# An encoder layer with grouped experts: the first expert's down rows split ahead of the second tile's columns, and three row tiles of the last norm finished on TensorE

## Chip, cores, metric

One Trainium2 chip, one core. The metric is the device time of the program in microseconds, the median of the runs.

## The reference

One layer of a hybrid encoder, 1024 tokens of width 1024, all in float32: a projection, a convolution branch and chunked attention, merged and projected, then a layer norm, then a mixture of experts and the last layer norm. The change touches the end alone:

```python
x = layer_norm(ALPHA * x + mixed, ln1_g[l], ln1_b[l])
x = layer_norm(ALPHA * x + grouped_moe(x, w_router, b_router, w_gate_up[l], w_down[l]),
               ln2_g[l], ln2_b[l])

def layer_norm(x, g, b):
    mu = jnp.mean(xf, axis=-1, keepdims=True)
    var = jnp.mean(jnp.square(xf - mu), axis=-1, keepdims=True)
    return ((xf - mu) * lax.rsqrt(var + LN_EPS)).astype(x.dtype) * g + b

# in grouped_moe: 16 experts, each token goes to 2 of them
    g, u = jnp.split(t @ w_gate_up[e], 2, axis=-1)
    out = out + combine[:, e:e + 1] * ((jax.nn.silu(g) * u) @ w_down[e])
```

## The kernel before, in words

All engines are programmed by hand, each with its own order of instructions, and meet at semaphores only. Matrices are multiplied in three products of float32 halves (a "high" part that ScalarE makes by a copy, and a "low" part that VectorE makes by subtracting the high one): high by high, high by low, low by high. Weights and activations are both split so.

**The experts.** The tokens of an expert are gathered in tiles of 128. A table `tab`, made by VectorE at run time (lines 1845 to 1855), says which expert each tile belongs to; here there are 21 tiles. `tables` (line 1862) says that it and the counts are there; `slots_ok` (line 1867) says that `w_slot` (each token's weight) and `to_i` (where its result is added) are, which are the last readers of memory that the down rows' buffers share. Every engine loads four counts into registers (`ends`, line 1235 and 1238 to 1241).

For tile i TensorE transposes the gathered rows (`transpose_x`, line 1505), multiplies the result for tile i-2 by the down weights (`down`, products of lines 1436 to 1438), transposes tile i-1's hidden values (`transpose_h`, line 1532) and multiplies by the gate and up weights (`up`, 8 chunks of rows by 3 x 2 products). The first tiles are written out one by one (lines 1561 to 1584). ScalarE copies the columns out (`x_t`, line 1634), scales the result (`y`, line 1670), copies the down rows' high part (`down_rows`, line 1645, 4 rows for each expert) and that of the transposed hidden values (`h_t`, 1651), then the next expert's gate rows (`gate_rows`, line 1330, 8 copies), then does silu (1661). VectorE follows it with the low parts (`x_t` 1790, `dn_l` 1875, `hbl` 1879, `gu` 1336) and the gate's product (`gate`, 1891).

In ScalarE's order before the change the first expert's `down_rows` stand in step(1), behind silu(0) (lines 1683 to 1690). In VectorE's order tile 1's `x_t` and three gate rows stand ahead of the slots (lines 1863 to 1867); the first `dn_l` stand in step(1), behind gate(0) and the last four gate rows (1903 to 1907).

SP loads weights in the order of lines 1304 to 1310: the gate and up rows of expert e+1 (1 MB pairs, each once the pair of two experts ago is used up), then, when `dn_lo` says that all four low parts of expert e-1 are made, the down rows of expert e (2 MB into `dn_raw`). GpSimd gathers tokens (line 1364) and adds results to memory (line 1374); it waits for `slots_ok` before its step(1) (1389 to 1391).

**The last norm.** SP reads the summed rows back in 8 row tiles (line 1318). For each, VectorE takes the mean from a column (`mean`, 1925), ScalarE squares with a sum (1710) and takes the root (1713), VectorE subtracts and multiplies by g (`scale_row`, 1932), takes the reciprocal (1938) and multiplies by it and adds b (`finish`, 1941). A ninth pass normalises the rows of the last expert tile, which VectorE adds from PSUM (`last_rows`, 1948) ahead of row tile 4; ScalarE takes their sum at its turn 6 (1708). SP stores the row tiles in order (1320 to 1321); when all are out and the ninth is ready GpSimd stores that one (1406 to 1409).

Of the kernel before, what the change touches and what calls it, by code (L numbers as in the profile page):

```python
# [13 lines left out]
P = 128  # L14
# [69 lines left out]
def encoder_layer(nc, xT, x, wblk, b_in, dw, dwb, lncg, lncb, relb, b_o, ln1_g, ln1_b,  # L84
# [5 lines left out]
    with ctx:  # L90
# [101 lines left out]
        ys2 = at("ys2", [P, D + 1], F32, 180.5)  # L192

# [990 lines left out]
def moe(nc, sem, m):  # L1184
# [7 lines left out]
     xf, g2_b, b2_b, rows_l, norm_l, ys2, squares, x1_tot, w_last, to_last, cst, eps2, st6, mv, rstd, nmr, wgt, ids_i, id_now, to_i, to_now, w_slot, tab, cum_i, ends_i, rows_i, br_b,  # L1192
     ps, psf, ident) = (m[k] for k in (
         "x1 x1t hot_a hot_b wr_t ones rt_a rt_b rank_a rank_b slot_i mh sums xgh2 xgl2 hot_0 both upto_t val wide tc id0 one_i init_p wo_add gu dn_h dn_l dn_raw xg xgh xgl hb hbh hbl ys "
         "xf g2_b b2_b rows_l norm_l ys2 squares x1_tot w_last to_last cst eps2 st6 mv rstd nmr wgt ids_i id_now to_i to_now w_slot tab cum_i ends_i rows_i br_b "
# [11 lines left out]
    idc = sem("idc"); toc = sem("toc"); to_set = sem("to_set"); slots_ok = sem("slots_ok"); id_set = sem("id_set"); gath = sem("gath")  # L1207
# [6 lines left out]
    tot_set = sem("tot_set"); f_tot = sem("f_tot"); f_nm = sem("f_nm"); f_sq = sem("f_sq"); f_sd = sem("f_sd")  # L1214
# [10 lines left out]
    logits_of = lambda a, z: ps[:, 6, (NE + 1) * a:(NE + 1) * z].rearrange("p (t e) -> p t e", e=NE + 1)  # L1225
    by_g = lambda a: a.rearrange("p (g e) -> p g e", e=EPG)
# [45 lines left out]
    def split_dn(i):  # L1272
        return {0: False, 1: True}.get(i) if isinstance(i, int) else None


    def place_of(e):

        return 1 - e % 2
# [13 lines left out]
    def sync_part(sp):  # L1292
        sp.wait_ge(x1_out, 16 * TT)
        sp.wait_ge(acc_out, 16 * TT)
        sp.wait_ge(xt_r, TT)
        load_gu(sp, 1, pairs=range(2, 4))
        sp.wait_ge(lg_done, TT)
        load_dn(sp, 0)

        sp.wait_ge(tot_set, 1)  # L1300
        sp.dma_start(acc_dram[0:SEQ, D:D + 1].rearrange("(t p) c -> p t c", p=P), x1_tot[:], allow_slow_non_contiguous=True).then_inc(acc_out, 16)
        sp.wait_ge(ids_done, 3)
        sp.wait_ge(tables, 1)
# [35 lines left out]
    def pool_part(pool):  # L1339
# [27 lines left out]
        def store(i, rows=ys[:]):  # L1367
# [5 lines left out]
            pool.sem_inc(to_set, 1)  # L1373
# [32 lines left out]
        pool.wait_ge(f_ok, TT + 1)  # L1406
# [198 lines left out]

    def halves(i):

        return [slice(HALF * h, HALF * h + HALF) for h in range(2)]
# [12 lines left out]
    def scalar_part(act):  # L1621
# [14 lines left out]
        def down_rows(i, first=False, before=None, rows=range(FC)):  # L1636
            e = 0 if first else load(act, T_E, i - 1)
            act.wait_ge(dn_in, e * 16 + 16)
            if first:

                act.wait_ge(slots_ok, 1)
            if not first:
                act.wait_ge(dn_done, i - 1 if before is None else before)
            for k in rows:
                act.activation(dn_h[:, k, :], dn_raw[:, k, :], ACT.Copy).then_inc(dn_hi, 1)  # L1645
# [26 lines left out]
        def step(i):  # L1672
# [5 lines left out]
            when(act, T_SPLIT_DN, i, split_dn(i), lambda: down_rows(i, first))  # L1678
# [6 lines left out]
        x_t(1)  # L1685
        act.wait_ge(tables, 1)
        total, end3, end2, end1 = ends(act)
        silu(0)
# [15 lines left out]
        for t in range(TT + 1):  # L1704
            if t == TT - 2:

                act.wait_ge(rows_ok, 1)
                act.activation(norm_l[:], rows_l[:, 0:D], ACT.Copy, accum_out=mv[:, TT, 0:1]).then_inc(f_tot, 1)
# [4 lines left out]
            act.activation(rstd[:, t:t + 1], mv[:, t, 1:2], ACT.Sqrt, scale=1.0 / D, bias=eps2[:]).then_inc(f_sd, 1)  # L1713

# [77 lines left out]
    def vector_part(dve):  # L1792
# [78 lines left out]
        def down_rows(i, first=False, rows=range(FC)):  # L1871
            e = 0 if first else load(dve, T_E, i - 1)
# [20 lines left out]
        def step(i):  # L1893
# [4 lines left out]
            when(dve, T_SPLIT_DN, i, split_dn(i), lambda: down_rows(i, static and i == 1))  # L1898
# [36 lines left out]
        def finish(t):  # L1935
# [3 lines left out]
            dve.wait_ge(f_rs, t + 1)  # L1939
            dve.wait_ge(f_g, t + 1)  # L1940
# [68 lines left out]
```

## Time and profile before

| | us |
|---|---|
| median of 3 runs (1184.24 to 1185.25) | 1184.93 |
| the profiled execution's own time | 1181.39 |
| its span | 1179.5 |
| TensorE busy | 1107.2 (94%) |
| VectorE, ScalarE busy | 817.9, 551.8 |
| `tables` made | 764.93 |
| first product of tile 1 | 774.91 |
| last product of the last tile begins | 1151.34 |
| last store is issued by GpSimd | 1173.54 |

PE is TensorE's products, PEld its weight loads, DVE is VectorE, ACT is ScalarE, POOL is GpSimd, SP is SyncE; a q behind a name is the engine's sequencer. A line of a timeline gives the start and the length in us, the engine, the source line, what is written and from what, how many instructions were merged, and in brackets the engine's idle time before it with what released it.

### The profile page before, as it was taken

What the parts mean: (1) busy time and instruction counts of PE and PEld (TensorE: products, weight loads), DVE (VectorE), ACT (ScalarE), POOL (GpSimd) and SP (SyncE); (2) the same over time, 40 slices, a digit from 0 to 9 for tenths busy, and PEclk for the clock granted to TensorE, in tenths of its full rate; (3) what the DMA queues carried; (4) which work ended last, traced back from release to release, by engine and by line L of the source; (5) the groups of instructions that cost most, each with busy time, mean ns of one, the idle gap of its engine ahead of it and who ended that gap; (6) DMA issues with size and microseconds to landing.
All of it is one profiled execution on the core that took longest, in us unless ns stands there. A gap on an engine that the chain in (4) does not pass through costs nothing.

```text
span 1179.5 us, 17089 instructions
## 1 busy us (share of the span) xinstructions
PE 1107.2 (94%) x5645; PEld 924.2 (78%) x5646; DVE 817.9 (69%) x1147; ACT 551.8 (47%) x814; POOL 93.0 (8%) x101
## 2 busy tenths in 40 slices
PE   7999999999999989899999999999999999999980
PEld 5888888879777778778788888778788888888760
DVE  5799999835365755566587478778678665458767
ACT  5111212233476755656333033358577555457753
POOL 0000000000000000000000000034112211112220
PEclk9999999999999999999999999799999999999985
DMA  6121332322201010071344135569999876799965
GB/s 255 54 90 45 107 92 87 108 96 66 72 19 41 19 41 1 36 289 69 129 165 161 72 143 200 182 259 383 330 308 392 312 234 217 251 331 337 351 208 218
DMA packets 49797, 199.58 MB, mean 169 GB/s; under 512 B 7248, under 2 KB 7632, under 8 KB 47680
## 3 DMA queue, kind: packets, MB, share of 16 engines
q1 hardware_dynamic: 43536, 176.19, 39.7%
q0 software_dynamic: 6192, 22.49, 7.8%
q8 instruction: 41, 0.67, 0.2%
q14 instruction: 28, 0.23, 0.1%
HBM read 166.21 MB, written 32.52 MB: 168 GB/s over the span
## 4 chain that ended last, share of the span: by engine, by line
PE 80%; DVE 6%; DMA 5%; ACT 4%; issue 4%; ACTq 0%; DVEq 0%; SPq 0%; POOL 0%; POOLq 0%
PE ps L469 17%; PE ps L471 16%; PE ps L470 16%; PE ps L1436 8%; PE ps L1438 8%; PE ps L1437 8%; DMA gu<-in_wexp 3%; PE ps L1505 1%; PE ps L1432 1%; PE ps L554 1%; PE ps L540 1%; ACT pr L801 1%; ACT pth L825 1%; DVE ptl L1043 1%; DVE xf L1932 1%
## 5 line engine op out<-in xcount | busy, mean ns | idle before, releaser
L469 PE MATMUL ps<-xh,wh 128*128 128x512 f32 x512 | 203.0, 396 | 12.2 <-DVE xl L905 8.1
L470 PE MATMUL ps<-xl,wh 128*128 128x512 f32 x512 | 200.0, 391 | 0.0
L471 PE MATMUL ps<-xh,wl 128*128 128x512 f32 x512 | 199.9, 390 | 0.0
L1336 DVE TENSOR_TENSOR gu<-gu (+1 forms) x128 | 148.6, 1220 | 34.8 <-issue 23.9
L928 DVE SCALAR_TENSOR_TENSOR cv<-u,dw_t,cv 128x1024 f32<-128x1024 f32 x120 | 154.1, 1284 | 3.7
L1436 PE MATMUL ps<-gu,xgh 128*128 x336 | 133.3, 397 | 2.0 <-DVE xgl L1790 2.0
L1330 ACT ACTIVATE gu<-gu (+1 forms) x128 | 124.4, 1048 | 21.1 <-DMA gu<-in_wexp 13.4
L1438 PE MATMUL ps<-gu,xgl 128*128 x336 | 131.1, 390 | 0.0
L1437 PE MATMUL ps<-gu,xgh 128*128 x336 | 130.8, 389 | 0.0
L469 PEld LDWEIGHTS ps<-xh,wh 128*128 128x128 f32 x512 | 96.5, 189 | 34.4 <-issue 14.4
L471 PEld LDWEIGHTS ps<-xh,wl 128*128 128x128 f32 x512 | 96.5, 188 | 20.4
L470 PEld LDWEIGHTS ps<-xl,wh 128*128 128x128 f32 x512 | 96.6, 189 | 19.8 <-issue 0.5
L900 DVE TENSOR_TENSOR wl<-raw,wh 128x1024 fp32r<-128x1024 f32 x52 | 63.5, 1223 | 55.3 <-ACT wh L732 55.2
L732 ACT ACTIVATE wh<-raw 128x1024 fp32r<-128x1024 f32 x52 | 54.5, 1056 | 97.0 <-DMA raw<-in_wblk 96.8
L1875 DVE TENSOR_TENSOR dn_l<-dn_raw,dn_h 128x1024 fp32r<-128x1024 f32 x64 | 74.2, 1220 | 11.9 <-ACT dn_h L1645 11.1
L1043 DVE TENSOR_TENSOR ptl<-ps,pth 128x512 fp32r<-128x512 f32 (+1 forms) x72 | 41.0, 597 | 57.3 <-ACT pth L825 57.3
L1436 PEld LDWEIGHTS ps<-gu,xgh 128*128 128x128 f32 x336 | 63.1, 188 | 15.6 <-issue 3.2
L1438 PEld LDWEIGHTS ps<-gu,xgl 128*128 128x128 f32 x336 | 63.1, 188 | 13.5
L1437 PEld LDWEIGHTS ps<-gu,xgh 128*128 128x128 f32 x336 | 63.2, 188 | 12.5
L1436 PE MATMUL ps<-dn_h,hbh 128*128 128x512 f32 x168 | 68.6, 408 | 3.3 <-DVE hbl L1879 3.3
L1437 PE MATMUL ps<-dn_l,hbh 128*128 128x512 f32 x168 | 66.9, 398 | 0.0
L1438 PE MATMUL ps<-dn_h,hbl 128*128 128x512 f32 x168 | 66.7, 397 | 0.0
(262 smaller groups left out, 2051.6 us busy)
## 6 DMA issues: line engine op xcount, KB each, us to landing
gu<-in_wexp SPq DMA_DIRECT2D x64, 1024.0 KB, 8.8
dn_raw<-in_wexp SPq DMA_DIRECT2D x16, 2048.0 KB
raw<-in_wblk SPq DMA_DIRECT2D x52, 512.0 KB, 3.9
gate_cols<-gst SPq DMA_DIRECT2D x16, 512.0 KB, 5.1
xf<-acc_rows SPq DMA_DIRECT2D x8, 512.5 KB, 8.2
xraw<-in_xT SPq DMA_DIRECT2D x8, 512.0 KB, 7.7
gcm<-gate_cols SPq DMA_DIRECT2D x8, 512.0 KB, 7.2
gam<-gate_cols SPq DMA_DIRECT2D x8, 512.0 KB, 14.6
```

What stands on the lines that cost most here:

```text
L469: pe.matmul(o, a_h, b_h, start=first, stop=False)
L470: pe.matmul(o, a_h, b_l, start=False, stop=False)
L471: return pe.matmul(o, a_l, b_h, start=False, stop=last)
L732: act.activation(hi, src, ACT.Copy).then_inc(w_hi, 1)
L900: dve.tensor_tensor(lo, src, hi, ALU.subtract).then_inc(w_lo, 1)
L928: dve.scalar_tensor_tensor(out=cv[:, j, :], in0=tap, scalar=w, in1=cv[:, j, :], op0=ALU.mult, op1=ALU.add).then_inc(conv_d, 1)
L1330: eng.activation(gu[:, par, k, 0, :], gu[:, par, k, 1, :].bitcast(F32), ACT.Copy).then_inc(gu_hi, 1)
L1336: eng.tensor_tensor(gu[:, par, k, 1, :], gu[:, par, k, 1, :].bitcast(F32), gu[:, par, k, 0, :], ALU.subtract).then_inc(gu_lo, 1)
L1436: pe.matmul(o, a_h, b_h, start=first, stop=False)
L1437: pe.matmul(o, a_h, b_l, start=False, stop=False)
L1438: return pe.matmul(o, a_l, b_h, start=False, stop=last)
L1875: dve.tensor_tensor(dn_l[:, k, :], dn_raw[:, k, :], dn_h[:, k, :], ALU.subtract).then_inc(dn_lo, 1)
```

## The change

It does two things. First, the first expert's down rows: ScalarE makes their high part behind the gate rows of expert 1 and ahead of tile 1's `x_t`, and also does a one-element Silu there; VectorE makes the slots ahead of the three gate rows, and dn_l row 0 ahead of tile 1's `x_t`, rows 1 to 3 where they stood. Second, the last norm: for row tiles 1, 3 and 5 VectorE's second pass is left out. It makes a diagonal matrix of the reciprocals, TensorE forms b plus diagonal times rows in PSUM, and ScalarE copies the result back into xf two turns later, from where SP stores it. Some semaphores change names with this.

```diff
+        diag = at("diag", [P, 3, P], F32, 185)
...
+    ON_PE = (1, 3, 5)
+    STORED = {t: n for n, t in enumerate(t for t in range(TT + 1) if t not in ON_PE)}
...
         for t in range(TT):
-            sp.wait_ge(f_ok, t + 1)
+            if t in ON_PE:
+                sp.wait_ge(tot_set, 2 + ON_PE.index(t))
+            else:
+                sp.wait_ge(f_ok, STORED[t] + 1)
             sp.dma_start(out[P * t:P * t + P, :], xf[:, t, 0:D]).then_inc(f_out, 16)
...
-            pool.sem_inc(to_set, 1)
+            pool.sem_inc(id_set, 1)
...
-        pool.wait_ge(f_ok, TT + 1)
+        pool.wait_ge(f_ok, STORED[TT] + 1)
...
         down(end1, by_row=True)
+        pe.wait_ge(ln2_in, 32)
+        for n, t in enumerate(ON_PE):
+            halves_of = [(ps[:, 2 * n + h, :], slice(HALF * h, HALF * h + HALF)) for h in range(2)]
+            for o, c in halves_of:
+                pe.matmul(o, ident, b2_b[:, c], start=True, stop=False)
+            pe.wait_ge(f_g, t + 1)
+            pe.wait_ge(diag_ok, n + 1)
+            for o, c in halves_of:
+                last = pe.matmul(o, diag[:, n, :], xf[:, t, c], start=False, stop=True)
+            last.then_inc(fin_done, 1)
...
# ScalarE
-            when(act, T_SPLIT_DN, i, split_dn(i), lambda: down_rows(i, first))
+            if not first:
+                when(act, T_SPLIT_DN, i, None, lambda: down_rows(i))
...
         x_t(0)
         gu_high(act, 1, place_of(1), range(6, KC))
-        x_t(1)
+        act.wait_ge(dn_in, 16)
+        act.wait_ge(slots_ok, 1)
+        for k in range(FC):
+            act.activation(dn_h[:, k, :], dn_raw[:, k, :], ACT.Copy).then_inc(dn_hi, 1)
         act.wait_ge(tables, 1)
         total, end3, end2, end1 = ends(act)
+        act.activation(st6[:, 0, 0, 1:2], eps2[:], ACT.Silu)
+        x_t(1)
         silu(0)
...
             act.activation(rstd[:, t:t + 1], mv[:, t, 1:2], ACT.Sqrt, scale=1.0 / D, bias=eps2[:]).then_inc(f_sd, 1)
+            if t - 2 in ON_PE:
+                n = ON_PE.index(t - 2)
+                act.wait_ge(fin_done, n + 1)
+                act.activation(xf[:, t - 2, 0:D], psf[:, D * n:D * n + D], ACT.Copy).then_inc(tot_set, 1)
...
# VectorE
         V.tensor_copy(cum_i[:], cum).then_inc(tables, 1)
-        gu_low(dve, 1, place_of(1), range(3))
-        x_t(dve, 1)
         link(V.tensor_copy(w_slot[:], ps[:, 5, TAB:2 * TAB]))
...
+        def first_down_rows(rows):
+            for k in rows:
+                dve.wait_ge(dn_hi, k + 1)
+                dve.tensor_tensor(dn_l[:, k, :], dn_raw[:, k, :], dn_h[:, k, :], ALU.subtract).then_inc(dn_lo, 1)
+        gu_low(dve, 1, place_of(1), range(3))
         dve.wait_ge(tables, 1)
         total, end3, end2, end1 = ends(dve)
+        first_down_rows(range(1))
+        x_t(dve, 1)
...
+            if static and i == 1:
+                first_down_rows(range(1, FC))
+            else:
+                when(dve, T_SPLIT_DN, i, None, lambda: down_rows(i))
...
             dve.wait_ge(f_rs, t + 1)
+            if t in ON_PE:
+                dve.tensor_scalar(diag[:, ON_PE.index(t), :], ident, rstd[:, t:t + 1], None, ALU.mult).then_inc(diag_ok, 1)
+                return
             dve.wait_ge(f_g, t + 1)
```

## Rows read from the trace of the kernel before

**Rows 1.** The page's chain that ended last: shares of the span by engine.

```profile
PE 80%; DVE 6%; DMA 5%; ACT 4%; issue 4%; ACTq 0%; DVEq 0%; SPq 0%; POOL 0%; POOLq 0%
```

**Rows 2.** Waits of TensorE, 772 to 1145: who for whom, us in total, times, longest.

```profile
PE ps L1532 <- DVE hb L1891: 4.6, 2, 3.3
PE ps L1436 <- DVE hbl L1879: 3.3, 2, 1.8
...
PE ps L1436 <- DVE xgl L1790: 2.0, 2, 1.2
```

**Rows 3.** Timeline of TensorE, 772 to 800 (columns as told above).

```profile
786.64 1.03 PE L1505 MATMUL ps<-ident_t,xg 128*128 128x128 f32 x8
789.52 0.66 PE L1436 MATMUL ps<-dn_h,hbh 128*128 128x512 f32 x1 [1.84 <-DVE hbl L1879]
789.98 0.63 PE L1437 MATMUL ps<-dn_l,hbh 128*128 128x512 f32 x1
...
796.46 0.39 PE L1438 MATMUL ps<-dn_h,hbl 128*128 128x512 f32 x1
```

**Rows 4.** Timeline of VectorE, 764 to 800.

```profile
765.02 3.49 DVE L1336 TENSOR_TENSOR gu<-gu 128x1024 fp32r<-128x1024 f32 x3
...
775.09 0.19 DVE L1867 SCALAR_TENSOR_TENSOR to_i<-ps,rt_b 128x32 int32<-128x32 f32 x1
...
779.61 4.62 DVE L1336 TENSOR_TENSOR gu<-gu 128x1024 fp32r<-128x1024 f32 x4
784.15 4.63 DVE L1875 TENSOR_TENSOR dn_l<-dn_raw,dn_h 128x1024 fp32r<-128x1024 f32 x4
788.70 0.69 DVE L1879 TENSOR_TENSOR hbl<-ps,hbh 128x512 fp32r<-128x512 f32 x1
```

**Rows 5.** Stretches: length, busy us of each engine (instructions), PEclk granted, DMA share, GB/s.

```profile
790.00:794.00 4.00, 4.00 (x13) 3.14 (x12) 4.00 (x5) 2.39 (x4) 4.00 (x1) 0.61 0.84 340
...
1152.00:1156.00 4.00, 0.00 (x0) 0.00 (x0) 3.96 (x7) 1.91 (x4) 0.00 (x0) 0.86 1.01 344
```

**Rows 6.** Timeline of VectorE, 1120 to 1182.

```profile
1151.59 1.29 DVE L1941 SCALAR_TENSOR_TENSOR xf<-xf,rstd,b_b 128x1024 f32<-128x1024 f32 x1
...
1171.28 1.28 DVE L1941 SCALAR_TENSOR_TENSOR norm_l<-norm_l,rstd,b_b 128x1024 f32<-128x1024 f32 x1
```

**Rows 7.** Chain that ended last, 1140 to 1180: start us, us, what.

```profile
1170.00 2.61 DMA out_rows<-xf
```

**Rows 8.** Timeline of ScalarE, 742 to 840.

```profile
772.75 1.09 ACT L1634 ACTIVATE xgh<-ps 128x512 fp32r<-128x512 f32 x2 [11.91 <-PE ps L1505]
775.14 1.28 ACT L1661 ACT_TABLE_LOAD   x1 [1.30 <-issue]
...
776.93 3.89 ACT L1645 ACTIVATE dn_h<-dn_raw 128x1024 fp32r<-128x1024 f32 x4
...
790.84 0.58 ACT L1661 ACTIVATE hb<-ps 128x512 f32<-128x512 f32 x1
```

**Rows 9.** Timeline of SP's DMA queue, 730 to 1180.

```profile
788.81 0.34 SPq L1290 DMA_DIRECT2D dn_raw<-in_wexp  x1
```

**Rows 10.** Chain that ended last, 740 to 860.

```profile
791.56 17.17 DMA gu<-in_wexp
808.81 21.50 DMA gu<-in_wexp
```

**Rows 11.** Timeline of ScalarE, 1120 to 1182, the change of table.

```profile
1143.31 1.28 ACT L1703 ACT_TABLE_LOAD   x1
```

**Rows 12.** Groups by form, VectorE and ScalarE: busy us, mean ns, idle before.

```profile
L1036 DVE TENSOR_SCALAR pr<-pr,rinv 128x128 f32<-128x128 f32 x4 | 1.1, 287 | 0.1
...
L1614 ACT ACTIVATE x1t<-ps 128x1024 f32<-128x1024 f32 x8 | 8.2, 1026 | 30.7 <-PE ps L1420 30.7
```

**Rows 13.** Line 508, TensorE: ns min/median/max, first and last start, forms.

```profile
L508 PE MATMUL ps<-csum,ones_c x4: 590/592/592, 249.2 to 250.5; 128*128 128x512 f32 x4
```

**Rows 14.** Timeline of ScalarE, 1120 to 1182, the norm.

```profile
1150.33 1.15 ACT L1710 ACTIVATE squares<-xf,nmr 128x1024 f32<-128x1024 f32 x1 [1.11 <-DVE nmr L1925]
```

More of the change, by code:

```diff
@@ L1191, in moe @@
     (x1, x1t, hot_a, hot_b, wr_t, ones, rt_a, rt_b, rank_a, rank_b, slot_i, mh, sums, xgh2, xgl2, hot_0, both, upto_t, val, wide, tc, id0, one_i, init_p, wo_add, gu, dn_h, dn_l, dn_raw, xg, xgh, xgl, hb, hbh, hbl, ys,
-     xf, g2_b, b2_b, rows_l, norm_l, ys2, squares, x1_tot, w_last, to_last, cst, eps2, st6, mv, rstd, nmr, wgt, ids_i, id_now, to_i, to_now, w_slot, tab, cum_i, ends_i, rows_i, br_b,
+     xf, g2_b, b2_b, rows_l, norm_l, ys2, diag, squares, x1_tot, w_last, to_last, cst, eps2, st6, mv, rstd, nmr, wgt, ids_i, id_now, to_i, to_now, w_slot, tab, cum_i, ends_i, rows_i, br_b,
      ps, psf, ident) = (m[k] for k in (
          "x1 x1t hot_a hot_b wr_t ones rt_a rt_b rank_a rank_b slot_i mh sums xgh2 xgl2 hot_0 both upto_t val wide tc id0 one_i init_p wo_add gu dn_h dn_l dn_raw xg xgh xgl hb hbh hbl ys "
-         "xf g2_b b2_b rows_l norm_l ys2 squares x1_tot w_last to_last cst eps2 st6 mv rstd nmr wgt ids_i id_now to_i to_now w_slot tab cum_i ends_i rows_i br_b "
+         "xf g2_b b2_b rows_l norm_l ys2 diag squares x1_tot w_last to_last cst eps2 st6 mv rstd nmr wgt ids_i id_now to_i to_now w_slot tab cum_i ends_i rows_i br_b "
          "ps psf ident").split())
@@ L1206, in moe @@
     tables = sem("tables"); ids_ok = sem("ids_ok"); id0_ok = sem("id0_ok"); sums_ok = sem("sums_ok")
-    idc = sem("idc"); toc = sem("toc"); to_set = sem("to_set"); slots_ok = sem("slots_ok"); id_set = sem("id_set"); gath = sem("gath")
+    idc = sem("idc"); toc = sem("toc"); diag_ok = sem("diag_ok"); slots_ok = sem("slots_ok"); id_set = sem("id_set"); gath = sem("gath")
     tx_done = sem("tx_done"); tx_hi = sem("tx_hi"); tx_lo = sem("tx_lo"); gu_rows = sem("gu_rows")
@@ L1213, in moe @@
     rows_in = sem("rows_in"); rows_ok = sem("rows_ok"); w_set = sem("w_set"); last_stored = sem("last_stored")
-    tot_set = sem("tot_set"); f_tot = sem("f_tot"); f_nm = sem("f_nm"); f_sq = sem("f_sq"); f_sd = sem("f_sd")
+    tot_set = sem("tot_set"); fin_done = sem("fin_done"); f_nm = sem("f_nm"); f_sq = sem("f_sq"); f_sd = sem("f_sd")
     f_rs = sem("f_rs"); f_g = sem("f_g"); f_ok = sem("f_ok"); f_out = sem("f_out")
@@ L1270, in split_gu @@
         return True if isinstance(i, int) and i == 0 else None
-    def split_dn(i):
-        return {0: False, 1: True}.get(i) if isinstance(i, int) else None
     def place_of(e):
@@ L1634, in x_t, with down_rows @@
                 act.activation(hi[:, c], psf[:, c], ACT.Copy).then_inc(tx_hi, 1)
-        def down_rows(i, first=False, before=None, rows=range(FC)):
-            e = 0 if first else load(act, T_E, i - 1)
+        def down_rows(i, before=None, rows=range(FC)):
+            e = load(act, T_E, i - 1)
             act.wait_ge(dn_in, e * 16 + 16)
[L1639 to L1643, printed above, removed]
+            act.wait_ge(dn_done, i - 1 if before is None else before)
             for k in rows:
@@ L1707, in scalar_part @@
                 act.wait_ge(rows_ok, 1)
-                act.activation(norm_l[:], rows_l[:, 0:D], ACT.Copy, accum_out=mv[:, TT, 0:1]).then_inc(f_tot, 1)
+                act.activation(norm_l[:], rows_l[:, 0:D], ACT.Copy, accum_out=mv[:, TT, 0:1]).then_inc(rows_ok, 1)
             act.wait_ge(f_nm, t + 1)
@@ L1867, in vector_part, with down_rows @@
         V.scalar_tensor_tensor(out=to_i[:], in0=ps[:, 5, 0:TAB], scalar=-1.0, in1=et, op0=ALU.add, op1=ALU.add).then_inc(slots_ok, 1)
+        def first_down_rows(rows):
[3 more added lines that the diff above has]
+        gu_low(dve, 1, place_of(1), range(3))
         dve.wait_ge(tables, 1)
         total, end3, end2, end1 = ends(dve)
-        def down_rows(i, first=False, rows=range(FC)):
-            e = 0 if first else load(dve, T_E, i - 1)
+        first_down_rows(range(1))
+        x_t(dve, 1)
+        def down_rows(i, rows=range(FC)):
+            e = load(dve, T_E, i - 1)
             for k in rows:
@@ L1897, in step @@
                 late_rows(i - 1)
-            when(dve, T_SPLIT_DN, i, split_dn(i), lambda: down_rows(i, static and i == 1))
+            if static and i == 1:
+                first_down_rows(range(1, FC))
+            else:
+                when(dve, T_SPLIT_DN, i, None, lambda: down_rows(i))
             h_t(i - 1)
@@ L1923, in mean @@
             else:
-                dve.wait_ge(f_tot, 1)
+                dve.wait_ge(rows_ok, 2)
             dve.tensor_scalar(nmr[:, t:t + 1], xf[:, t, D:D + 1] if t < TT else mv[:, t, 0:1], -1.0 / D, None, ALU.mult).then_inc(f_nm, 1)
```

## The prediction

> **What bounds the kernel now.** The page's chain of waits comes first: TensorE holds 80% of it, so time is to be had only where TensorE stops, or where the chain leaves it [rows 1]. TensorE's own waits between 772 and 1145 us say where it stops: 4.6 us on hb, 3.3 us on hbl, 2.0 us on xgl, in all of it; of the hb waits 3.3 us are at 1141, on the last tile, the other at 832 [rows 2]. The change touches two places.
>
> The first is the first product with an expert's down rows. TensorE ends tile 2's transposes at 787.5 and begins down(0) at 789.52 after 1.84 us idle [rows 3]. It waits for hbl, which VectorE makes at 788.70, behind four dn_l subtractions of 784.15 to 788.7 [rows 4]. The stop also costs the clock: the granted clock is 0.61 of full speed over 790 to 794 [rows 5], and the first products start 0.43 us apart (789.52 to 789.98 and on), while the last 15 of the 24 start 0.228 us apart, up to 796.46 [rows 3].
>
> The second is the last norm. VectorE never rests from 1147.5 to 1172.5: two passes of 1.28 us a row tile, 2.65 us a tile in all [rows 6]. TensorE is done at 1151.7. The end is the last of those passes, together with the store of row tile 7, 2.61 us from 1170.00 [rows 7].
>
> **Part 1, the down rows.** ScalarE's four copies (3.89 us from 776.93) leave the place behind silu(0), for the idle time ahead of tile 1's columns, which reach it at 772.75 [rows 8]. They wait for the slots; those were written at 775.09 because they stood behind three subtractions and x_t(1) [rows 4]. Moved ahead of these, right behind the tables at 765.0, the three short instructions end at about 765.7, and the copies run from 765.8 to 769.7. Four register loads follow (some 1.3 us are seen between x_t(1) and the table load), then the Silu table load of 1.28 us, which no longer stands ahead of silu(0), then a one-element Silu of 0.2 us: ready at 772.5, with 0.2 us left to x_t(1) [rows 8]. Cover is thin; were it gone, TensorE has still 0.9 us, since it starts tile 1 at 774.91 for its own register loads.
>
> VectorE: slots to 765.7, three subtractions (3.49 us) to 769.2, register loads to 770.8, dn_l row 0 to 772.0, x_t(1) at 773.4 as before, the subtraction of gate row 3 at 774.7, gate(0) at 775.8, four subtractions to 781.0, dn_l rows 1 to 3 to 784.5, hbl done at 785.2 instead of 789.4 [rows 4]. TensorE therefore finds everything ready when its transposes end at 787.5. It gains 787.5 against 789.52, 2.0 us, and full speed for the 24 products: they took 789.52 to 796.69, 7.2 us, and take 24 x 0.227 = 5.4 us [rows 3]. That is 3.7 us at TensorE. What is late next is silu(1) at 790.84, held by ScalarE's eight copies for the next expert and not moved [rows 8]; gate(1) is then done at 792.2 and TensorE wants it at 792.9, so it costs nothing, by 0.7 us. GpSimd waits for the slots as well, so its gather for tile 2 comes some 4 us earlier; nobody wants it before 786.64. Its renamed semaphore costs nothing.
>
> On SP's queue the load of expert 1's down rows waits for all four dn_l: 784.6 instead of 788.81, and the loads for expert 3 behind it move too, by about 4 us [rows 9]. This matters: the chain passes through those loads for 17.17 and 21.50 us, up to the hb stop of 832 [rows 10]. They must come 3.7 us earlier, or that stop takes the gain back. The first does. The down rows of expert 2 need a buffer that VectorE now frees at about 803.0, only 1.8 us earlier: it waits for silu(1) and then pays 1.7 us of register loads. But the queue still holds the end of expert 3's rows until about 804.7 then, so it hardly runs dry. I take 3.4 us for part 1; bounds are 1.8 us (the queue follows its latest trigger) and 4.2 us (all of the DMA's lead, the stop at 832 shrinking too). Beyond it TensorE is busy and only shifts.
>
> Does a table load take more than its 1.28 us? The one of 1143.31, right behind a copy, has no idle time ahead of it [rows 11]; the one of 775.14 has 1.30 us [rows 8], which I put down to the four register loads there. The Trainium skill (ScalarE: Activation LUTs, What ACT_TABLE_LOAD costs) says that a switch costs a drain of about 1.4 us beside the load; by it part 1 would be worth about 0.4 us less. Rows 11 show no such drain, and the sum goes by them.
>
> **Part 2, the norm.** Row tiles 1, 3, 5 lose VectorE's second pass, 1.20 us of its time each (its 1.28 us overlap the next) [rows 6], and get a 128x128 tensor_scalar, 0.29 us by the nearest row and 0.20 us back to back [rows 12]. Three times 1.0 is 3.0 us less for VectorE.
>
> TensorE, idle there, does two products of ident and b2_b and two of diag and the rows, per row tile. They are true fp32, and such a product of 512 columns is two recorded instructions that start 0.43 us apart (four between 249.2 and 250.5) at full clock [rows 13]: 8 x 0.43 = 3.5 us a row tile. Straight behind the last down product: row tile 1 at 1155.2, row tile 3 at 1158.7, row tile 5, whose diag is ready at about 1161.9, at 1163.7. (These times leave out the shift by part 1.)
>
> ScalarE gets three copies from PSUM of 1.03 us [rows 12] beside its 1.76 us a row tile (square 1.15 us, sum, root) [rows 14]. Walked through: copy 1 waits for TensorE until 1155.2 and ends at 1156.2; square(4) is done at 1157.5, just when VectorE, behind last_rows, wants it. Then copy 3, the copy with a sum for the last rows and square(6) follow one another, and VectorE waits about 1.0 us for square(6), at 1161.8 to 1162.8. With that VectorE ends at about 1170.7 instead of 1172.5: 1.9 us. The stores are the other leg. SP issues in order, so store 1 now waits for copy 1 (1156.2) with stores 2 to 4 behind it; that is early enough. Store 5 waits for copy 5 (1165.6) with 6 behind it and 7 at 1168.2; at about 1.3 us each they are out at 1170.8. If TensorE's wait for the third diag, about 1.6 us, loses the clock as 1.84 us did at 789.5 [rows 3, 5], copy 5 is 0.9 us later, three stores stand together and the end is 1171.6. I take 1.6 us; bounds are 3.0 us gained (no wait of ScalarE) and 0.3 us gained (both legs worse).
>
> **Sum.** 3.4 + 1.6 = 5.0 us. The profiled execution took 1181.39 us (span 1179.5), 3.5 us under the median of the three runs, 1184.93: it becomes 1176.4, and the median 1179.9.
>
> **Rivals.**
> A. *The loads don't follow.* The stop at 832 ends by DMA, and expert 2's down rows leave only 1.8 us earlier. Part 1 is then 1.8: 1181.5 in the median. For: the chain through the loads [rows 10]. Against: they queue behind a transfer still in flight. Chance 0.13.
> B. *The gain of part 1 is absorbed*, the gathers and accumulating stores of GpSimd now meeting the loads in another order: 1.6 us alone, 1183.3. Against: a busy DMA that starts 4 us earlier also ends earlier. Chance 0.12.
> C. *The table load comes too late.* If the 1.30 us ahead of the old one belong to it and not to the register loads [rows 8], it now ends near 774.0, x_t(1) starts 1.3 us late, and TensorE, with 0.9 us in hand, loses 0.4 us: 1180.3. That is what the cited section would do here. Rows 11 speak against it. Chance 0.05.
> D. *ScalarE becomes the bound of the norm* and eats all of part 2: 1181.5. Chance 0.04.
> E. *The norm gets slower.* ScalarE stands in order behind TensorE. If the new products ran at half clock, 7 us a row tile, copies 1, 3, 5 would end at 1159.6, 1166.5 and 1173.6, and the norm at 1176.9: 4.3 us slower than before, 0.9 us with part 1, 1185.8. It decides from the point where part 1 is under 4.3 us; with its low bound the kernel is 2.5 us slower. For: over 1152 to 1156 the clock falls, mean 0.86 [rows 5]. Against: there TensorE had nothing to do, here it goes on without a gap. Chance 0.08.
> That the change does not do what it says I see no way to.
>
> **Chances and range.** The forecast has 0.58. Measured against no change, 0.2% or 2.4 us is what can be told. Forecast, A, C, D lie beyond it on the fast side (0.80); B and half of E lie within (0.16); the other half of E is slower (0.04). The range goes from the high bounds, 4.2 + 3.0 us gained, and 0.7 us by which the lowest run lies under the median, 1177.0, to B's 1183.3.
>
> **What would show it.** Right: dn_h copies at 766 and the table load near 771.2 on ScalarE; slots at 765.5; hbl by 785.3; no wait of TensorE ahead of down(0) and clock 1.0 over 790 to 794; the hb stop near 828.6 not longer than before; VectorE's norm some 1.9 us shorter with one wait of about 1 us for square(6). Wrong: x_t(1) after 773.1, a longer hb stop, clock 0.5 under the fp32 products, or a last store that lands more than 0.5 us behind VectorE's end.

## The result, and the profile after

The changed kernel takes 1176.37 us in the median of 9 runs (1173.54 to 1180.91). Nine runs of the kernel before, the three known and six taken beside it, have a median of 1182.36 (1181.11 to 1185.25), 6.0 us more. The ratio is 0.994, 95% interval 0.993 to 0.9951, which is 5.8 to 8.3 us. All three known runs lie above all six taken beside the changed kernel (1181.11 to 1183.49, median 1181.84); against these six alone the medians differ by 5.5 us. The same pair was run twice more, each time on one chip, as after_again and after_third below: 0.9963 [0.9948, 0.9978] and 0.9962 [0.9949, 0.9975], medians 4.6 and 4.9 us apart. The forecast was 1179.9 with a range from 1177.0: the measured median lies 3.5 us under the forecast and 0.6 us outside the range. The profiled execution took 1176.37 us with a span of 1174.5, 5.0 us less than the span of before.

The page's chain by engine now reads (to be held against [rows 1]):

```profile
PE 81%; DVE 6%; ACT 5%; DMA 5%; issue 3%; DVEq 0%; ACTq 0%; POOL 0%; SPq 0%; POOLq 0%
```

TensorE's waits, 772 to 1145 us (who for whom, us in total, times, longest; against [rows 2]):

```profile
PE ps L1538 <- DVE hb L1924: 3.6, 1, 3.6
PE ps L1511 <- issue: 2.4, 1, 2.4
PE ps L1442 <- DVE xgl L1816: 2.0, 2, 1.2
PE ps L1442 <- DVE hbl L1912: 1.5, 1, 1.5
```

The two hb stops of before ended at 834 and 1141.5; one is left, on the last tile, and hbl has lost the 1.8 us stop ahead of down(0). Timeline of TensorE at that place (start, us, engine, line, operation; against [rows 3]):

```profile
786.17 1.03 PE L1511 MATMUL ps<-ident_t,xg 128*128 128x128 f32 x8
786.96 0.48 PE L1442 MATMUL ps<-dn_h,hbh 128*128 128x512 f32 x1
787.27 0.40 PE L1443 MATMUL ps<-dn_l,hbh 128*128 128x512 f32 x1
...
792.27 0.39 PE L1444 MATMUL ps<-dn_h,hbl 128*128 128x512 f32 x1
```

The first product follows the transposes with no idle time, and the 24 start 0.23 us apart from the second on. Timeline of VectorE in the changed kernel (against [rows 4]):

```profile
765.27 0.19 DVE L1891 SCALAR_TENSOR_TENSOR to_i<-ps,rt_b 128x32 int32<-128x32 f32 x1
765.37 3.49 DVE L1342 TENSOR_TENSOR gu<-gu 128x1024 fp32r<-128x1024 f32 x3
768.78 1.22 DVE L1896 TENSOR_TENSOR dn_l<-dn_raw,dn_h 128x1024 fp32r<-128x1024 f32 x1
...
780.64 3.49 DVE L1896 TENSOR_TENSOR dn_l<-dn_raw,dn_h 128x1024 fp32r<-128x1024 f32 x3
784.04 0.68 DVE L1912 TENSOR_TENSOR hbl<-ps,hbh 128x512 fp32r<-128x512 f32 x1
784.64 5.75 DVE L1342 TENSOR_TENSOR gu<-gu  x5
```

Timeline of its ScalarE (against [rows 8]):

```profile
769.48 1.28 ACT L1708 ACT_TABLE_LOAD   x1
770.77 0.20 ACT L1708 ACTIVATE st<-eps 128x1 f32<-128x1 f32 x1
772.53 1.09 ACT L1652 ACTIVATE xgh<-ps 128x512 fp32r<-128x512 f32 x2 [1.55 <-PE ps L1511]
773.90 0.60 ACT L1675 ACTIVATE hb<-ps 128x512 f32<-128x512 f32 x1 [0.29 <-PE ps L1444]
...
790.38 0.57 ACT L1675 ACTIVATE hb<-ps 128x512 f32<-128x512 f32 x1
```

Timeline of its SP queue (against [rows 9]):

```profile
784.15 0.34 SPq L1292 DMA_DIRECT2D dn_raw<-in_wexp  x1
785.18 2.16 SPq L1289 DMA_DIRECT2D gu<-in_wexp  x4
802.30 0.34 SPq L1292 DMA_DIRECT2D dn_raw<-in_wexp  x1
```

ScalarE is idle 1.55 us behind the table load and the small Silu; it waits for TensorE, not for the table. The split of h ends at 784.7, 2.2 us before TensorE wants it. Windows (length, busy us of PE, PEld, DVE, ACT, POOL with instructions, granted clock, DMA share, GB/s; against [rows 5]):

```profile
790.00:794.00 4.00, 3.87 (x19) 3.06 (x18) 2.28 (x4) 3.12 (x6) 1.59 (x3) 1.00 0.98 402
1152.00:1156.00 4.00, 4.00 (x11) 1.55 (x10) 3.96 (x7) 3.61 (x6) 0.00 (x0) 1.00 0.83 337
1160.00:1164.00 4.00, 1.15 (x3) 0.19 (x1) 3.93 (x7) 3.71 (x7) 0.00 (x0) 1.00 0.44 173
```

The norm. Timeline of VectorE in the changed kernel (against [rows 6]):

```profile
1153.27 0.29 DVE L1977 TENSOR_SCALAR diag<-ident_t,rstd 128x128 f32<-128x128 f32 x1
...
1159.59 1.29 DVE L1968 SCALAR_TENSOR_TENSOR xf<-xf,nmr,g_b 128x1024 f32<-128x1024 f32 x1 [0.48 <-ACT squares L1732]
...
1166.22 1.28 DVE L1980 SCALAR_TENSOR_TENSOR norm_l<-norm_l,rstd,b_b 128x1024 f32<-128x1024 f32 x1
```

Timeline of its ScalarE (against [rows 14]), the first and the last copy out of PSUM:

```profile
1152.05 1.03 ACT L1739 ACTIVATE xf<-ps 128x1024 f32<-128x1024 f32 x1 [1.13 <-PE ps L1620]
...
1161.18 1.03 ACT L1739 ACTIVATE xf<-ps 128x1024 f32<-128x1024 f32 x1
```

Timeline of its TensorE, which had nothing to do there before:

```profile
1148.41 1.88 PE L1616 MATMUL ps<-b_b,ident_t 128*128 128x512 f32 x4
1150.13 1.88 PE L1620 MATMUL ps<-xf,diag 128*128 128x512 f32 x4
...
1155.50 1.88 PE L1616 MATMUL ps<-b_b,ident_t 128*128 128x512 f32 x4
1159.19 1.96 PE L1620 MATMUL ps<-xf,diag 128*128 128x512 f32 x4 [1.81 <-DVE diag L1977]
```

**A ledger by stages.** For every kernel the same stretches were read from the timelines: Tn is the start of tile n's transposes on TensorE, "mean" the first instruction of the norm on VectorE, "issue" the issue of the last row's store on GpSimd, 5.95 to 6.05 us before the end of the span. T20, the last tile, lies in the stretch to the mean; "clk T20" is the granted clock in the microsecond from its start. Values in us, one profiled execution each; "after" stands there three times (after, after_again, after_third).

```
kernel        T1-T3  T3-T5  T1-T5  T5-T19  T19-mean  mean-issue  clk T20
before        36.58  38.28  74.86  247.89  51.57     27.54       1.00
p2_only       36.58  39.85  76.43  248.52  52.05     25.14       1.00
after         32.79  37.82  70.61  247.92  53.39     25.12       0.50
after_again   32.82  38.42  71.24  247.94  52.18     26.27       1.00
after_third   32.78  38.59  71.37  247.90  52.09     25.15       1.00
p1_only       32.77  38.58  71.35  247.90  52.02     27.54       1.00
dve_only      34.66  41.29  75.95  248.22  53.95     26.06       0.58
hold_dn       33.03  41.50  74.53  247.89  52.51     25.12       1.00
late_store    32.77  43.69  76.46  247.89  52.63     25.16       1.00
early_dn      33.00  35.50  68.50  247.89  52.67     26.04       1.00
warm          32.78  37.60  70.38  247.89  55.62     25.49       0.50
best          32.79  37.45  70.24  247.88  52.39     25.14       1.00
no_preload    32.83  40.63  73.46  247.89  53.57     26.08       0.50
two_tiles     32.78  37.95  70.73  248.19  53.19     25.54       0.52
```

From T5 to T19 nothing moves by more than 0.7 us. Part 1 acts between T1 and T5, part 2 behind the first mean. Two other things move the rows. What lies ahead of T1 differs by up to 4.0 us (T1 at 771.22 to 775.21), for a reason not traced. And TensorE's clock is lost in some executions and kept in others. In the nine where the last tile's transposes ran at a granted 1.00, T19 to the mean is 51.6 to 52.7 us; in the four where they ran at 0.50 to 0.58, 53.2 to 54.0 (warm, with more work there, 55.6). The changed kernel stands on both sides, after and after_again. T3 to T5 holds such losses too: p2_only had a mean of 0.57 over 839.8 to 843.8, no_preload 0.58 over 832.3 to 836.3, each behind two stops of 1.2 us, while the kernel before kept 1.00 behind stops of 1.26 and 1.16 us. So one profile can't tell differences under some 2 us in these two stretches. The stretches carry the argument, and the ratios are the check.

### The profile page after: what moved, and what is told of

Read it like the earlier page. It is cut to its first block, busy times and chain, and to the rows that moved or that the text cites. A ratio compares the mean times of both kernels' runs of the same rounds, so it can differ in the third digit from the quotient of the medians.

```text
span 1174.5 us, 17141 instructions
## 1 busy us (share of the span) xinstructions
PE 1116.6 (95%) x5669; PEld 928.4 (79%) x5670; DVE 814.9 (69%) x1147; ACT 554.7 (47%) x818; POOL 87.0 (7%) x101
## 4 chain that ended last, share of the span: by engine, by line
PE 81%; DVE 6%; ACT 5%; DMA 5%; issue 3%; DVEq 0%; ACTq 0%; POOL 0%; SPq 0%; POOLq 0%
PE ps L470 17%; PE ps L472 16%; PE ps L471 16%; PE ps L1442 8%; PE ps L1444 8%; PE ps L1443 8%; DMA gu<-in_wexp 3%; PE ps L1511 1%; PE ps L1438 1%; PE ps L555 1%; PE ps L541 1%; ACT pr L802 1%; ACT pth L826 1%; DVE ptl L1044 1%; DVE pr L1021 1%
## 5 line engine op out<-in xcount | busy, mean ns | idle before, releaser
L470 PE MATMUL ps<-xh,wh 128*128 128x512 f32 x512 | 202.8, 396 | 12.3 <-DVE xl L906 8.1
L1908 DVE TENSOR_TENSOR dn_l<-dn_raw,dn_h 128x1024 fp32r<-128x1024 f32 x60 | 69.6, 1219 | 11.4 <-ACT dn_h L1659 10.5
```

The lines of the kernel that those rows point to most:

```text
L470: pe.matmul(o, a_h, b_h, start=first, stop=False)
L1908: dve.tensor_tensor(dn_l[:, k, :], dn_raw[:, k, :], dn_h[:, k, :], ALU.subtract).then_inc(dn_lo, 1)
```

## The experiments

**Each part alone.** p1_only takes the diagonal, TensorE's products and ScalarE's copies out of the norm; p2_only puts the first expert's down rows back on both engines (ScalarE as in dve_only below):

```diff
 p1_only, in scale_row (and the products and copies that go with it)
-            if t in ON_PE:
-                dve.tensor_scalar(diag[:, ON_PE.index(t), :], ident, rstd[:, t:t + 1], None, ALU.mult).then_inc(diag_ok, 1)
-                return
 p2_only, VectorE
+        gu_low(dve, 1, place_of(1), range(3))
+        x_t(dve, 1)
         link(V.tensor_copy(w_slot[:], ps[:, 5, TAB:2 * TAB]))
...
-        gu_low(dve, 1, place_of(1), range(3))
-        first_down_rows(range(1))
-        x_t(dve, 1)
```

> Part 1 alone (the first expert's down rows; the norm as before). Theory 1, the two parts add up and part 1 is worth what the two traces show between them once the start of the experts is set equal (transposes of tile 3 and on come 4.2 us earlier): 4.2 us faster than before, 1178.2 against 1182.4. Rival, the gain is lost again at the stop of 1112, which the changed kernel had longer and with a lost clock (the lead shrank from 4.4 to 2.6 us there): 2.5 us faster. In its trace hbl by 785.3 and no stop ahead of down(0) either way; they differ in the lead left at the last tile's transposes.

Measured: 0.9966 [0.9952, 0.998], 1179.93 us beside 1183.7 of before. T1 to T5 71.35, 3.5 us less than before; the norm is unchanged. The interval reaches from 2.4 to 5.7 us and so leaves both expectations standing; in the profile 0.5 us of the lead is gone again between T19 and the mean, not the 1.7 that the rival needs.

> Part 2 alone (three row tiles of the norm finished on TensorE; everything at the start of the experts as before). Theory 1: the stretch from the first mean to the end of VectorE's last pass is 24.1 us instead of 26.6, so 2.4 us faster than before. Rival, part 2 gained more only because the last down product ended earlier at a better clock in the one changed execution: 1.6 us faster, as forecast, with ScalarE's copy 1 later and a wait of about 1 us for square(6).

Measured: 0.9966 [0.9953, 0.9979], 1180.18 us. Mean to issue 25.1 instead of 27.5. The two ratios multiply to 0.9932: inside the interval of the first comparison, below those of the two later ones, so the ratios don't show that the whole is the full sum. The stretches do: after_third has p1_only's T1 to T5 (71.37 and 71.35) and p2_only's norm (25.15 and 25.14). Neither part absorbs the other. T1 to T5 runs here through the code of before and took 76.43 us, 1.6 more than in the profile of before, with the clock lost as told above.

**Are ScalarE's copies needed?** dve_only keeps the order of VectorE and of the slots, but gives the four dn_h copies back to their place behind silu(0), the dn_l rows with them:

```diff
 ScalarE
+        x_t(1)
         act.wait_ge(tables, 1)
...
-        act.activation(st6[:, 0, 0, 1:2], eps2[:], ACT.Silu)
-        x_t(1)
 VectorE
-        first_down_rows(range(1))
...
-                first_down_rows(range(1, FC))
+                first_down_rows(range(FC))
```

> The changed kernel with ScalarE's order as it was (down rows and table load behind tile 1's columns); VectorE has the slots and its register loads ahead of the three gate rows, and all four dn_l where they stood. Theory 1, what counts is that VectorE's order is 3.5 us shorter in front of hbl: silu(0) ends at 777.0 as before, hbl comes at about 787, TensorE stops 0.3 us at most ahead of down(0) and keeps its clock, but the down rows of expert 1 are asked for at 786.7 instead of 784.2, so the stop of 829 is 1.5 to 2.5 us longer: 2 us slower than the changed kernel, 2 us faster than part 2 alone. Rival A, ScalarE's early copies are what counts: no gain over part 2 alone. Rival B, the order of the loads is without effect: within 0.5 us of the changed kernel.

Measured: 0.9988 [0.9977, 1.0], 1183.1 us. T1 to T3 34.66: half of the early gain. T3 to T5 41.29: 3 us lost, by something that no theory had. TensorE waits 2.8 us for hbl, and ScalarE's waits, 772 to 850, name what is behind it:

```profile
ACT ys L1692 <- DMA acc_rows<-ys,to_now: 9.4, 1, 9.4
```

y(1) may not write its buffer until the accumulating store of tile 0 has landed, and that store is late at GpSimd; the chain that ended last in dve_only passes through it, 15.95 us from 803.72. Timeline of GpSimd in dve_only:

```profile
787.52 5.60 POOL L1371 COPY id_now<-ids_i 128x1 int32<-128x1 int32 x1 [12.84 <-PE ps L1515]
793.90 0.96 POOL L1374 DMA_INDIRECT xg<-x_rows,id_now  x1 [0.79 <-POOL id_now L1371]
794.86 7.99 POOL L1380 COPY to_now<-to_i 128x1 int32<-128x1 int32 x1
803.72 6.86 POOL L1384 DMA_INDIRECT acc_rows<-ys,to_now  x1 [0.86 <-POOL to_now L1380]
```

Timeline of GpSimd in the kernel before:

```profile
789.61 6.28 POOL L1364 DMA_INDIRECT xg<-x_rows,id_now  x1 [0.79 <-POOL id_now L1361]
795.90 0.19 POOL L1370 COPY to_now<-to_i 128x1 int32<-128x1 int32 x1
798.92 7.37 POOL L1374 DMA_INDIRECT acc_rows<-ys,to_now  x1 [2.83 <-ACT ys L1670]
```

Timeline of ScalarE in the kernel before, y(1) behind that store:

```profile
816.54 1.12 ACT L1670 ACTIVATE ys<-ps,w_slot 128x1024 f32<-128x1024 f32 x1 [4.20 <-DMA acc_rows<-ys,to_now]
```

Timeline of GpSimd in the changed kernel:

```profile
787.34 3.10 POOL L1367 COPY id_now<-ids_i 128x1 int32<-128x1 int32 x1 [12.85 <-PE ps L1511]
...
794.73 2.22 POOL L1380 DMA_INDIRECT acc_rows<-ys,to_now  x1 [2.35 <-ACT ys L1684]
```

A copy of one column takes 0.19 us or 8 us. The long ones end with VectorE's run of subtractions with both inputs in SBUF: in after the copy ends at 790.44 and the run of 784.64 (above) at 790.39; in dve_only the two copies end at 793.12 and 802.85, the runs at 793.07 and 802.81. In before the issue of the store took 7.37 us, and y(1) waited 4.2 us for its landing; in after it took 2.22, and y(1) does not wait. The change takes this wait away too, which the prediction did not see. What that is worth is another matter: in before the chain passes through the two loads at this time [rows 10], not through the store.

**Are the loads needed?** hold_dn keeps all, but SP asks for expert 1's down rows only behind TensorE's third set of transposes, so that the loads behind it are late as well:

```diff
             if e == 1:
+                sp.wait_ge(tx_done, 3)
```

> The changed kernel, but SP asks for expert 1's down rows only once TensorE has transposed tile 2 (at 787.2 instead of 784.15), with the loads for expert 3 behind it. Theory 1, the loads' lead is what lets TensorE keep its gain: the chain through the loads ends 3.1 us later, the stop near 829 grows by 2.5 to 3.1 us, the kernel is 2.5 to 3 us slower than the changed one. Rival, the gain is TensorE's alone and the queue makes up for it: under 0.7 us slower.

Measured: 0.9979 [0.9966, 0.9993], 1181.15 us. Counted from T1 the load is asked 3.3 us later (at 790.26, T1 at 774.26; in after 784.15 and 771.46). T1 to T3 keeps its gain, 33.03, and T3 to T5 gives it back, 41.50 against 37.8 to 38.6, by a stop on hb at 816 with a clock of 0.50 to 0.66 for 8 us behind it. The chain comes to that stop through a load of 19.57 us from 793.02. TensorE's timeline in hold_dn:

```profile
816.00 1.11 PE L1540 MATMUL ps<-ident_t,hb 128*128 128x128 f32 x4 [2.22 <-DVE hb L1926]
```

So the gain at down(0) is kept only if the loads come earlier with it: this is rival A, with its cause forced. The price is less sure than the path. The ratio stands 0.0016 to 0.0039 above those of the changed kernel, which were taken on other chips, 1.9 to 4.6 us, and the intervals overlap two of the three.

**Is GpSimd's late store enough to lose it?** late_store holds the store of tile 0 back until silu(2), everything else as changed; after_again is the changed kernel beside it:

```diff
-        step(2)
+        pool.wait_ge(tx_done, 3)
+        gather(3)
+        pool.wait_ge(silu_ok, 3)
+        store(0)
```

> The changed kernel, but GpSimd holds the store of tile 0's result until silu(2) is done (about 809 instead of 794.7). In the kernel before, GpSimd's gather and this store stood 6.3 and 7.4 us in their issue, each until a row of VectorE's subtractions had ended, and the store landed so late that ScalarE's y(1) waited 4.2 us for it; in the changed kernel that wait is gone. Theory 3, this is the part of the gain that the forecast did not have: with the store held, y(1) waits to about 820, the down rows behind it are late, TensorE stops 2.5 to 3 us ahead of down(2), as it did with ScalarE's old order, and the kernel is about 3 us slower than the changed one. Rival, the loads alone set the stop of 829: under 0.7 us slower.

> The changed kernel once more, beside its variants on the same chip. By all theories 0.993 to 0.995 of before, with the stretch from tile 1's transposes to tile 5's at 70.6 us (74.9 before), and GpSimd's first store issued in about 2.2 us.

Measured: late_store 0.9993 [0.9979, 1.0007], 1183.18 us; after_again 0.9963 [0.9948, 0.9978], 1178.52 us. T3 to T5 43.69 against 38.42. y(1) waits 12.3 us for the store and TensorE stops 4.55 us for hbl; TensorE's timeline in late_store:

```profile
828.47 0.77 PE L1445 MATMUL ps<-dn_h,hbh 128*128 128x512 f32 x1 [4.55 <-DVE hbl L1915]
```

The two intervals don't overlap: held back this far, one store costs the whole of part 1. A wait for the store alone doesn't: in early_dn, next, y(2) waited 4.60 us for one (GpSimd's one-column copy ahead of it took 7.93 us), and T3 to T5 was the shortest of all.

**More of the same.** early_dn makes the last three dn_l rows right behind gate(0), ahead of the four gate and up subtractions, so that SP may ask for the loads earlier:

```diff
-            if static and i == 1:
-                first_down_rows(range(1, FC))
-            else:
+            if not (static and i == 1):
...
         gate(0)
+        first_down_rows(range(1, FC))
```

> The changed kernel with dn_l rows 1 to 3 right behind gate(0), ahead of the last four gate rows, so that expert 1's down rows can be asked for at about 779.6 instead of 784.15. TensorE wants gate row 4 at 780.9 and gets it at 780.6, the others 0.6 us or more ahead of need. Theory 1, the loads' lead still counts: the stop of 829 (hb late, 1.2 us on xgl and the end of the transposes) shrinks, 1 to 2 us faster than the changed kernel. Rival, the load for expert 3 still waits for TensorE at 786 and the rest of the queue is as before: within 0.5 us. A miss would be gate row 4 or 5 late, a stop of up to 1 us at 781.

Measured: 0.9936 [0.9922, 0.995], 1176.23 us; T3 to T5 35.50, 2.9 us less than in after_again on the same chip (medians 2.3 us apart, intervals overlapping), with one wait of TensorE, 0.9 us on xgl, left from T1 to T5. The down rows are asked for 8.2 us behind T1 (781.41 and 773.25), in after 12.7. In best, below, the same code gave 37.45 in its profile, with the stops back (0.34 and 1.19 us), 0.4 us under the shortest of the changed kernel: what the place is worth is not settled.

**The clock of the last tile.** TensorE idles 2.1 to 2.4 us ahead of the last tile's transposes in every kernel (the issue wait above). TensorE's timeline in after:

```profile
1110.39 1.97 PE L1511 MATMUL ps<-ident_t,xg 128*128 128x128 f32 x8 [2.41 <-issue]
```

and in early_dn:

```profile
1109.93 1.09 PE L1511 MATMUL ps<-ident_t,xg 128*128 128x128 f32 x8 [2.42 <-issue]
```

The idle time is the same and the clock is not. warm puts seven products of no use there:

```diff
+        for _ in range(7):
+            pe.matmul(ps[:, 5, :], xgh[:, 0:P], xgh[:, HALF:D], start=True, stop=True)
```

> The changed kernel with seven products of no use (3 of 4 columns' halves of the last columns by themselves, into a PSUM bank that nobody reads) ahead of the last tile's transposes, where TensorE stands 2.4 us for the gather and in the profiled execution then ran at half clock. Theory, the clock lost there is what spreads the changed kernel's runs (1173.5 to 1180.9): the transposes at full clock in every execution, median 0.5 to 1.5 us lower, spread smaller. Rival, the clock is lost in the later stops anyway, no difference within 0.5 us.

Measured: 0.9946 [0.993, 0.9962], 1176.8 us. T19 to the mean came out 3.4 us longer in its profile than in after_again (55.62 against 52.18). The seven products start only behind the idle time (2.16 us, and the chain has it as issue, not as the gather), run at half clock and take the transposes' place. TensorE's timeline in warm:

```profile
1112.14 2.82 PE L1600 MATMUL ps<-xgh 128*128 128x512 f32 x7 [2.16 <-issue]
1114.76 1.74 PE L1511 MATMUL ps<-ident_t,xg 128*128 128x128 f32 x8
```

So the theory's "full clock in every execution" is false. The median is 1.7 us under after_again, with overlapping intervals: whether the edit helps in other executions is not shown.

**The last four, on one chip.** best is early_dn with ScalarE's copy of row tile 1 behind square(4) instead of ahead of it; after_third the changed kernel; no_preload without the small Silu; two_tiles with row tiles 1 and 3 alone on TensorE:

```diff
 best
-            if t - 2 in ON_PE:
-                n = ON_PE.index(t - 2)
+            if t in (4, 5, 7):
+                n = (4, 5, 7).index(t)
 no_preload
-        act.activation(st6[:, 0, 0, 1:2], eps2[:], ACT.Silu)
 two_tiles
-    ON_PE = (1, 3, 5)
+    ON_PE = (1, 3)
```

> The changed kernel with two edits: the first expert's last three down rows on VectorE right behind gate(0) (as in early_dn), and ScalarE's copy of row tile 1 out of PSUM one turn later, behind square(4) instead of ahead of it. Theory (ScalarE's copy of row tile 1 stands waiting for TensorE, and square(4) behind it holds VectorE for up to 1.03 us): VectorE waits for no square(4), the first mean to the last row's store issue is 25.1 us or less (26.1 in early_dn), T1 to T5 stays at 68.5 us; 1 to 3 us faster than the changed kernel, ratio to the kernel before 0.992 to 0.993. Rival (the copy only meets the next wait: TensorE's third product, and the output stores start later): first mean to issue stays at 26 us and the kernel is no faster than early_dn, 0.994.

Measured: 0.9938 [0.9926, 0.9949], 1175.14 us, 2.2 us under after_third. VectorE waits for no square(4); its only wait behind the norm's first is the 0.48 us for square(6). Mean to issue 25.14, where early_dn had 26.04. The same instruction in VectorE's timeline of early_dn:

```profile
1154.55 1.28 DVE L1967 SCALAR_TENSOR_TENSOR xf<-xf,nmr,g_b 128x1024 f32<-128x1024 f32 x1 [0.80 <-ACT squares L1732]
```

and in that of best:

```profile
1153.19 1.27 DVE L1967 SCALAR_TENSOR_TENSOR xf<-xf,nmr,g_b 128x1024 f32<-128x1024 f32 x1
```

The expected 68.5 us from T1 to T5 did not come (70.24). Its median is the lowest, but early_dn's ratio on another chip is as low (0.9936): which of the two is faster is not shown.

> The changed kernel itself again, as the reference on this chip for the three others. Ratio to the kernel before 0.994 to 0.996; T1 to T5 70.6 to 71.3 us; first mean to last issue 25.1 to 26.2 us.

Measured: 0.9962 [0.9949, 0.9975], 1177.37 us.

> The changed kernel without the small Silu that loads ScalarE's table ahead: the load goes back ahead of silu(0). Theory (its 1.3 us lies on the way from the gathered columns to silu(0)): silu(0), gate(0) and the six copies that free the next gate and up rows come about 1.3 us later; the columns of the second tile 1.3 us earlier on ScalarE; the loads are asked about 1.3 us later. Split of h still ends ahead of TensorE's need at 787 us, so T1 to T3 stays near 33 us, and what is lost is up to 1.3 us in T3 to T5 by the loads: ratio 0.995 to 0.997, up to 1.5 us slower than the changed kernel. Rival (the load's place is covered wholly): within 0.3 us of it.

Measured: 0.9962 [0.995, 0.9974], 1178.49 us: no difference that the ratios show. The load stands ahead of silu(0) again, and silu(0) starts at 774.94 instead of 773.90, but gate(0) hardly moves, 775.57 against 775.50, since VectorE is busy with the subtraction of gate row 3 until then. ScalarE's timeline in no_preload:

```profile
773.65 1.28 ACT L1675 ACT_TABLE_LOAD   x1
774.94 0.60 ACT L1675 ACTIVATE hb<-ps 128x512 f32<-128x512 f32 x1
```

VectorE's timeline in no_preload:

```profile
774.38 1.22 DVE L1342 TENSOR_TENSOR gu<-gu 128x1024 fp32r<-128x1024 f32 x1
775.57 0.69 DVE L1923 TENSOR_TENSOR hb<-hb,ps 128x512 f32<-128x512 f32 x1
```

T1 to T3 is the same (32.83) and the loads are asked at the same time; T3 to T5 was 2 us longer than in after_third, with the stop on hb at 1.21 instead of 0.79 us and the clock lost behind it, as told at the ledger. The ratios are equal, with some 2 us of room. The theory fell at its first step, gate(0) is not later, and its rival stands: the load's place is covered.

> The changed kernel with two row tiles of the norm (1 and 3) finished on TensorE instead of three. Theory (each tile moved takes 1.0 us off VectorE, which sets the end): row tile 5 costs VectorE its 1.3 us pass again less the 0.3 us diagonal; first mean to last issue 26.1 us instead of 25.1, 1 us slower than the changed kernel in that stretch. Rival (ScalarE and TensorE already hold the third tile back, so that it brings nothing): 25.1 to 25.3 us, and no difference.

Measured: 0.9967 [0.9955, 0.998], 1178.42 us. Mean to issue 25.5: VectorE has no wait left behind its first in the norm, so of the third tile's 1.0 us half is already given back in the wait for square(6). The third tile is worth 0.4 us, between the two expectations.

## Why the prediction came out wrong in its number

**The step that failed is the level in the sum**: the 1184.93 us of three runs from which the 5.0 us were taken, and the 0.7 us that the range allowed for it. The six runs beside the changed kernel have a median of 1181.84: 3.1 of the 3.5 us. The other 0.5 us is the gain, 5.5 instead of 5.0 us there, and 4.6 and 4.9 in the later comparisons. (By the pooled nine it is 2.6 and 1.0 us.) The warning stood in the prediction itself: the profiled execution of before took 1181.39, 3.5 us under that median and outside the three runs, and the range's low end did not use it. As a ratio the forecast was 1179.9 / 1184.93 = 0.9958: above the interval of the first comparison (up to 0.9951), and inside both later ones. Why the three runs stood higher is not known.

**A hit that was luck.** The prediction had the profiled execution at 1176.4, and it took 1176.37. By the ledger the two parts gave 4.25 and 2.42 us in it, 6.7 instead of 5.0, T1 came 0.2 us earlier, and 1.8 us were lost between T19 and the mean. Of these some 1.2 us went with the clock of the last tile, since after_again and after_third, which kept it, are shorter there by that much.

**Part 1, right in its steps, 0.1 to 0.9 us small.** Forecast against trace: slots 765.7, written at 765.27 to 765.46; hbl ready 785.2, done at 784.72; no stop ahead of down(0), none; clock 1.0 over 790 to 794, 1.00; loads asked at 784.6, the down rows at 784.15. T1 to T3 is the term of 3.7 us: it came out at 3.8 in all kernels that have the whole of part 1 but hold_dn and early_dn (3.6). From T1 to T5 part 1 gave 4.25, 3.6 and 3.5 us in the three profiles of the changed kernel against the profile of before, and 3.5 in p1_only: the 3.4 that the loads were to leave is within 0.2 us of three of the four. T3 to T5 hardly moved (38.28 before; 37.82, 38.42, 38.59), so the loads came earlier by as much as TensorE did, and not by more; the stop on hb, 1.26 us before, was 0, 0.7 and 0.8. The stretch of before is itself one execution, and p2_only's was 1.6 us longer. What the prediction missed is GpSimd: the copy or issue that stands through VectorE's subtractions, and y(1) waiting 4.2 us for the store in the old order. late_store and dve_only show that this leg can set the pace, early_dn that a wait of 4.6 us need not; that it brought anything in the change itself is not shown.

**Part 2, right in its walk, 1.6 forecast, 1.3 to 2.4 measured.** VectorE's 3.0 us came: in the first profile 2.4 of them are left, 0.48 us gone into the wait for square(6) that the walk had at 1.0. Copies at 1.00 to 1.03 us, products 1.72 us for four (3.5 us a row tile), diagonals 0.29 us are as priced. TensorE's end lay 5.0 us behind the first mean (1143.38 to 1148.41) instead of 5.7, and square(4) made VectorE wait for nothing there. The other profiles bear this out: with ScalarE's copy where the change has it and TensorE's end up to 5.5 us behind the mean there was no wait for square(4), at 5.8 us (warm) one of 0.26 us, at 6.3 to 6.6 us (after_again, early_dn, no_preload, dve_only) 0.8 to 1.0 us, and 1.3 to 1.5 us were gained. Part 2 hangs on where TensorE ends against the mean.

**The rivals.** A, the loads do not follow: did not come, but hold_dn shows that it is real. B, absorbed by GpSimd's transfers in another order: did not come; only dve_only and late_store lose by the store. C, the table load late: did not come; it stood right behind the fourth copy with no idle time, and ScalarE had 1.55 us over; even back in its old place (no_preload) it costs nothing that the ratios show. The rule of the Trainium skill that rival C rested on (ScalarE: Activation LUTs, What ACT_TABLE_LOAD costs), a drain beside the load, shows in no row here. D, ScalarE bounds the norm: in part, as the waits of 0.5 to 1.5 us, and priced in. E, the new products at half clock: did not come; the granted clock was 1.00 from 1148 to 1164, also behind the 1.81 us wait for the third diagonal.

## What to carry to other kernels

Work moved into an engine's idle time paid here only because the transfers behind it were asked earlier as well; read what each queue waits for, and hold one back to see what the lead is worth. Before splitting passes off the last engine, ask what then orders them: here one copy, waiting for a third engine in the middle of ScalarE's order, cost up to 1 us, and one turn later it cost nothing. And put a range around the baseline too: three runs stood 3.1 us over the next six, and the profiled execution had said so. When two profiles differ in a stretch that the change does not touch, look at the granted clock there first.

## What was not expected of the hardware

**GpSimd stands while VectorE subtracts.** One-column copies and the issue of indirect transfers take 0.2 to 1.6 us each where undisturbed. In the 14 profiles 34 of them took 2.9 to 9.0 us, all of them met by a back-to-back run of VectorE subtractions on two SBUF tiles: the 29 copies ended within 0.05 us of the run's end, the 5 issues 0.8 or 1.5 us behind it, about their own time (the gather of 789.61 ends at 795.89, the run at 795.06). Not every issue stands: others that began inside a run took 2.0 to 2.6 us and ended 2 to 5 us before its end, as the one of 794.73. What decides between the two is not shown. The Trainium skill (GPSIMD Engine Reference, Specifications) has GpSimd share its SBUF interfaces with VectorE and names two SBUF inputs as a case of contention; the traces agree and add the size, here up to a whole run of 8 us.

**The clock after a wait.** TensorE idled 1.84 us ahead of down(0) and the mean granted clock was 0.61 behind it [rows 3, 5]; it idled 1.81 us ahead of the third diagonal's products and the clock stayed at 1.00. Ahead of the last tile's transposes (in warm, of the seven products) it idled 2.1 to 2.4 us in all 14 profiles; the clock was lost in five of them and kept in nine, in the same code both ways. So here the length of the idle time alone does not decide it. What does was not tried.
